# Spreading the small matmuls of a merged projection over more of its tiles

## The chip, the cores and the metric

The kernel runs on one core of a Trainium2 chip. Its engines are TensorE (PE), VectorE (DVE), ScalarE (ACT), GpSimd (POOL) and SyncE (SP, which issues the DMAs here). They run their own instruction streams and meet at semaphores. The metric is the time of one execution on the device in microseconds; before the change its median is 2121.88 us over 3 runs (2121.46 to 2122.12).

## The reference

Two transformer-like blocks follow each other on an input of 256 tokens by 1024 features. The second has two layers. Each starts with a layer norm and a mixer of three parts (SSD, RWKV-7 and gated linear attention), all fed by one projection `x @ w_in`; a mixture of experts follows. The part at stake is the projection with the RWKV mixer:

```python
def hybrid_mixer(x, w_in, ...):
    p = x @ w_in
    s_z, s_xbc, s_dt, rw, gq, gk, gv, gg, ga = _split(p, IN_SPLITS_2)
...
def rwkv7_mixer(p, mu, w0, w2, a0, a2, g2, k_k, k_a, r_k, ln_g, ln_b):
    prev = jnp.pad(p, ((0, 0), (1, 0), (0, 0)))[:, :seq]
    p = p + (prev - p) * mu
...
    def step(state, inp):
        r_t, w_t, k_t, v_t, kk_t, a_t = inp
        sa = jnp.einsum('bhvk,bhk->bhv', state, -kk_t)
        state = (state * w_t[:, :, None, :] + sa[..., None] * (kk_t * a_t)[:, :, None, :]
                 + v_t[..., None] * k_t[:, :, None, :])
        return state, jnp.einsum('bhvk,bhk->bhv', state, r_t)
```

## The kernel before, in words

The stage at stake is `stage_mix2` (L1254). It stands in a hardware loop over the two layers, so it runs twice; I call the runs the first and the second pass. The first starts near 646 us of the span, the second near 1380. Before and behind it all engines meet at a barrier.

**The projection.** The output features are cut into 24 tiles (units), in the order LOW, K0, K1, R0, R1, V0, V1, GA, GQ, GK, GG0, GG1, X0 to X0+5, TOKA, TOKB, Z0 to Z0+3. The first 12 are plain fp32: 8 matmuls of 128x128 by 128x256 (L1897). From X0 on, weights and input are split into a high and a low part, and a tile is 24 matmuls (L1900). Weights come through a ring of 4 buffers (`Units`): SP loads, ACT rounds to the high part (`round`, L1227), DVE subtracts for the low part (`rest`, L1233).

**The RWKV recurrence** is computed in chunks of 32 tokens by small matmuls. `products` (L1699) makes the masked products of the vectors of a chunk. `squares` (L1724, L1727) and `inverse` (L1738) build the inverse of a triangular 32x32 matrix per chunk and head by repeated squaring; DVE adds each update (L1405) and ACT copies each power. `transposes` (L1709) turns vectors to token order. `through` (L1746) applies the inverse. `states_and_ends` (L1765, L1768, L1771) and `read_out` (L1788, L1791, L1793) prepare the step from chunk to chunk, `state` (L1806, L1813) does the seven steps. `heads64` (L1687) sums over the 64 features of a head.

**The order** is written by hand. Each engine has a function `after(u)`: what it does behind tile u. PE runs tile u, then its `after(u)`, then tile u+1, and so on; the small matmuls of one `after` stand in one piece between two tiles. Only three updates of the state stand in the middle of a tile: `state(2)`, `state(4)`, `state(6)` in X0+3, X0+4, X0+5. ACT copies each tile out of PSUM (`copied`), and two banks take turns, so tile u waits for the copy of tile u-2.

**What depends on what.** `inverse(j)` needs power j+1 copied by ACT and update j-1 added by DVE. `through` into W1 and W2 needs update 3. The states need both copies of W (`w_copied`), one by ACT (L1637), one by DVE (L1486). The read-out needs Q and E, which DVE makes behind the states (L1494, L1497). State c needs DVE's state c-1 (L1412).

Of the kernel before, what the change touches and what calls it, by code (L numbers as in the profile page):

```python
# [22 lines left out]
ALU = mybir.AluOpType  # L23
# [6 lines left out]
DT = D // P  # L30
# [1223 lines left out]
def stage_mix2(nc, k, L, w_dram, v_dram, ln_dram, lr_dram, wa2_dram, vecs, b, y):  # L1254
# [6 lines left out]
    with Stage(nc, "mix2") as st:  # L1261
# [88 lines left out]
        with nc.Block() as block:  # L1350
# [16 lines left out]
            def _(dve):  # L1367
# [49 lines left out]
                def after(u):  # L1417
# [38 lines left out]
                    elif u == V1_:  # L1456
                        mask(2, mM[:, 0], "c_above")
# [4 lines left out]
                    elif u == GA:  # L1462
                        inverse(0)
# [3 lines left out]
                    elif u == GQ:  # L1467
                        inverse(1)
# [6 lines left out]
                    elif u == GK:  # L1475
                        inverse(2)
                        dve.wait_ge(masked_done, 5)
                        mask(3, mM[:, 1], "c_upto")
                        mask(4, mM[:, 2], "c_upto")
                    elif u == GG0:  # L1480
                        inverse(3)
                        dve.wait_ge(bonus_done, 1)
                        ch.link(dve.tensor_tensor(flat(v_), ps[:, 2], flat(v_), ALU.mult))
                    elif u == GG1:
                        dve.wait_ge(w_done, 1)
                        dve.tensor_copy(W12[:, 1].rearrange("p b h c -> p (b h c)"), ps[:, 5]).then_inc(w_copied, 1)  # L1486
# [3 lines left out]
                        ch.link(dve.tensor_scalar(x1[:], x1[:], 1.0 / 16, None, ALU.mult))  # L1490
                        dve.tensor_tensor_scan(gcum[:], k.c("keep")[:, 0:S], x1[:], 0.0, ALU.mult, ALU.add).then_inc(cums_ready, 1)
                    elif u == X0:
                        dve.wait_ge(qe_done, 1)
# [7 lines left out]
                    elif u == X0 + 1:  # L1501
# [4 lines left out]
                    elif u == X0 + 2:  # L1506
# [4 lines left out]
                    elif u == X0 + 3:  # L1511
                        state(2)
                        for t in range(2):
                            ins = dve.tensor_scalar(v_[:, t], v_[:, t], vec("ln_b", t), None, ALU.add)
                        ch.link(ins)
                        dve.wait_ge(gate_copied, 1)
                        dve.tensor_tensor(v_, v_, gg[:], ALU.mult).then_inc(vb_ready, 1)
                        state(3)
                    elif u == X0 + 4:
                        state(4)  # L1520
                        dve.wait_ge(vb_ready, 1)
                        for t in range(2):
                            dve.tensor_scalar(gg[:, t], gg[:, t], vec("ln_g", t), None, ALU.mult).then_inc(vb_ready, 1)
# [1352 lines left out]
```

## Time and profile before

| what | value |
|---|---|
| median of the runs | 2121.88 us |
| the profiled execution, its own time | 2135.11 us |
| its span, first to last instruction | 2133.8 us |
| PE busy | 1892.1 us, 89% |
| DVE busy | 830.4 us, 39% |
| ACT busy | 635.1 us, 30% |
| DMA, mean | 253 GB/s |
| stage of the change, first pass | about 646 to 791.5 us |
| stage of the change, second pass | about 1380 to 1532.5 us |

PE's busy time counts pipelined matmuls from start to modelled end, so a gap between two rows is real idle time while a busy row is not full speed. "issue" as a releaser means that the engine waited for nothing that the profile shows. PEclk is the clock that was granted to TensorE, 1.00 for 2.4 GHz, 0.50 for 1.2 GHz. The line numbers are those of the kernel before; in the kernel after, L1897 is L1898 and L1900 is L1901, and the lines of the helpers are 3 lower.

### The profile page before, as it was taken

The page shows a single profiled execution, that of the slowest core. Times are in us where ns is not written, and L with a number is a line of the kernel's source. Part 1 is how long each engine was busy: PE and PEld are TensorE (multiplying, and loading weights), DVE is VectorE, ACT ScalarE, POOL GpSimd, SP SyncE. Part 2 cuts the span into 40 slices and gives each one's busy share as a digit, 9 for nine tenths or more (in the row PEclk, how much of TensorE's full clock was granted, in tenths as well). Part 3 has the DMA queues.
Part 4 walks back from the last instruction along what each step waited for, and adds up shares of the span by engine and source line. Part 5 has one row for each costly group of instructions (what it writes and reads, how often), then busy time and mean ns, then how long its engine had stood idle before and what let it go on. Part 6 is the DMA issues. An engine that isn't in the chain of part 4 may idle for free. (4 is left out here: it accounts for less than half of the span.)

```text
span 2133.8 us, 41370 instructions
## 1 busy us (share of the span) xinstructions
PE 1892.1 (89%) x17744; PEld 1332.8 (62%) x17744; DVE 830.4 (39%) x1665; ACT 635.1 (30%) x1197; POOL 52.1 (2%) x58
## 2 busy tenths in 40 slices
PE   7999998999987886789999999588866999999995
PEld 6889998889986784644444444267855444444432
DVE  5766666666654375521111111233745111111112
ACT  4554445554433232311111111132423111111112
POOL 0400000400000000000000000000000000000000
PEclk9999999999998997799999999888977999999998
DMA  6235553345513312699999999422117999999992
GB/s 262 100 139 184 192 181 132 110 149 193 182 60 103 101 42 79 260 383 426 429 428 428 428 428 428 190 80 92 31 80 308 384 427 428 428 428 428 430 426 115
DMA packets 52332, 540.00 MB, mean 253 GB/s; under 512 B 6576, under 2 KB 7760, under 8 KB 14672
## 3 DMA queue, kind: packets, MB, share of 16 engines
q1 hardware_dynamic: 52176, 537.80, 63.0%
q8 instruction: 113, 1.85, 0.4%
q14 instruction: 43, 0.35, 0.1%
HBM read 536.73 MB, written 1.05 MB: 252 GB/s over the span
## 5 line engine op out<-in xcount | busy, mean ns | idle before, releaser
L2668 PE MATMUL experts_psG<-weights_gu,experts_xc 128*64 128x512 f32 x2048 | 454.5, 593 | 19.5 <-DMA weights_gu<-in_moe_up 19.5
L2668 PEld LDWEIGHTS experts_psG<-weights_gu,experts_xc 128*64 128x64 f32 x2048 | 146.9, 137 | 315.6 <-issue 277.2
L422 DVE TENSOR_TENSOR ring_low<-ring_raw,ring_high 128x1024 fp32r<-128x1024 f32 x180 | 224.3, 1248 | 158.3 <-ACT ring_high L416 158.2
L2693 PE MATMUL experts_psD<-weights_d,experts_hT 128*64 128x512 f32 x1024 | 233.9, 598 | 1.6 <-ACT experts_hT L2629 1.6
L416 ACT ACTIVATE ring_high<-ring_raw 128x1024 fp32r<-128x1024 f32 x180 | 189.1, 1054 | 155.0 <-PE ffn_ps L539 91.3
L537 PE MATMUL ffn_ps<-first_x_high,ring_high 128*128 128x256 f32 x704 | 199.0, 283 | 0.1
L2599 DVE SCALAR_TENSOR_TENSOR experts_yc_low<-experts_psD,experts_slot_gate,experts_yc_high 128x512 fp32r<-128x512 f32 x64 | 48.0, 751 | 387.7 <-ACT experts_yc_high L2632 387.7
L539 PE MATMUL ffn_ps<-first_x_high,ring_low 128*128 128x256 f32 x704 | 198.6, 282 | 0.0
L538 PE MATMUL ffn_ps<-first_x_low,ring_high 128*128 128x256 f32 x704 | 198.0, 281 | 0.0
L2589 DVE TENSOR_TENSOR experts_sig<-experts_sig,experts_psG 128x256 f32<-128x256 f32 x64 | 27.0, 421 | 370.0 <-ACT experts_sig L2620 370.0
L2620 ACT ACTIVATE experts_sig<-experts_psG 128x256 f32<-128x256 f32 x64 | 24.6, 384 | 420.1 <-PE experts_psG L2668 420.1
L2693 PEld LDWEIGHTS experts_psD<-weights_d,experts_hT 128*64 128x64 f32 x1024 | 68.4, 136 | 119.4 <-issue 111.2
L538 PEld LDWEIGHTS ffn_ps<-first_x_low,ring_high 128*128 128x128 f32 x704 | 134.2, 191 | 0.1
L537 PEld LDWEIGHTS ffn_ps<-first_x_high,ring_high 128*128 128x128 f32 x704 | 133.4, 189 | 0.9 <-issue 0.9
L539 PEld LDWEIGHTS ffn_ps<-first_x_high,ring_low 128*128 128x128 f32 x704 | 133.8, 190 | 0.0
L2632 ACT ACTIVATE experts_yc_high<-experts_psD,experts_slot_gate 128x512 fp32r<-128x512 f32 x64 | 44.0, 687 | 263.4 <-PE experts_psD L2693 263.4
L1897 PE MATMUL mix_ps<-x_resid,mix_w_raw 128*128 128x256 f32 x384 | 100.7, 424 | 14.4 <-issue 9.9
L2644 PE MATMUL experts_psX<-experts_selb,parts_x 128*128 128x64 bf16 x3072 | 102.2, 194 | 10.8 <-DVE experts_gate_e L2569 10.8
L2644 PEld LDWEIGHTS experts_psX<-experts_selb,parts_x 128*128 128x128 bf16 x3072 | 95.7, 99 | 11.0 <-DVE experts_gate_e L2569 11.0
L1897 PEld LDWEIGHTS mix_ps<-x_resid,mix_w_raw 128*128 128x128 f32 x384 | 81.8, 216 | 30.2 <-issue 17.0
L529 PE MATMUL ffn_ps<-ffn_act_high,ring_low 128*128 128x256 f32 x352 | 98.6, 280 | 0.0
L527 PE MATMUL ffn_ps<-ffn_act_high,ring_high 128*128 128x256 f32 x352 | 98.2, 279 | 0.0
(487 smaller groups left out, 3234.0 us busy)
## 6 DMA issues: line engine op xcount, KB each, us to landing
weights_gu<-in_moe_gate SPq DMA_DIRECT2D x64, 2048.0 KB, 25.1
weights_gu<-in_moe_up SPq DMA_DIRECT2D x64, 2048.0 KB, 29.5
weights_d<-in_moe_down SPq DMA_DIRECT2D x64, 2048.0 KB, 28.4
ring_raw<-in_w SPq DMA_DIRECT2D x90, 1024.0 KB, 4.9
mix_w_raw<-in_w_in SPq DMA_DIRECT2D x44, 512.0 KB, 3.7
output_w_raw<-in_w_out SPq DMA_DIRECT2D x8, 1024.0 KB, 8.1
mix_w_raw<-in_w_in SPq DMA_DIRECT2D x4, 528.0 KB, 5.4
const<-in_const SPq DMA_DIRECT2D x1, 1344.0 KB, 17.7
```

The costliest lines, as they stand in the source:

```text
L416: act.activation(self.high[:, n % AHEAD], self.raw_half(n), ACT.Copy).then_inc(self.rounded, 1)
L422: dve.tensor_tensor(self.low[:, n % AHEAD], self.raw_half(n), self.high[:, n % AHEAD], ALU.subtract)\
L527: pe.matmul(out, w[0][:, kk], high, start=False, stop=False)
L529: return pe.matmul(out, w[1][:, kk], high, start=False, stop=stop)
L537: pe.matmul(out, w[0][:, kk], f.high[:, kk], start=kk == 0, stop=False)
L538: pe.matmul(out, w[0][:, kk], f.low[:, kk], start=False, stop=False)
L539: ins = pe.matmul(out, w[1][:, kk], f.high[:, kk], start=False, stop=kk == DT - 1)
L1897: return pe.matmul(out, a, c, start=kc == 0, stop=kc == DT - 1)
L2599: dve.scalar_tensor_tensor(yc_low[:], psD[:], slot_gate[:, par:par + 1], yc_high[:], ALU.mult, ALU.subtract)\
L2644: ins = pe.matmul(psX[:, t * SLOTS:(t + 1) * SLOTS], m.parts[:, i, blk, t * P:(t + 1) * P], selb[:, par, blk, 0:SLOTS], start=i == 0 and b ...
L2668: ins = pe.matmul(out, xc[:, kk], wgu[:, place, kk, :, j * S:(j + 1) * S], start=kk == 0, stop=kk == DT - 1)
L2693: ins = pe.matmul(psD[rows, :], hT[:, c, j * SLOTS:(j + 1) * SLOTS], wd[:, place, 2 * j + c, i * 512:(i + 1) * 512], start=j == 0 and c == ...
```

## The change

Two things move. The pieces of the recurrence are handed out to the tiles anew, most of them one tile later: `products(2)` and `mask(2)`, the four updates of the inverse, `products(4)`, the last two transposes, `through`, the states, the read-out, all state steps and the normalization behind them. And a function `within(u)` is new: what PE does in the middle of tile u. It takes `products(2)` (GA), `inverse(0)` to `inverse(3)` (GQ, GK, GG0, GG1), the first half of `states_and_ends` (X0+1) and the three even state steps. DVE and ACT follow in their `after` functions. No operation is added or dropped. PE's part of the diff:

```diff
@@ tensor
-                def states_and_ends():
+                def states_and_ends(ns):
                     pe.wait_ge(w_copied, 2)
-                    for n in range(NP):
+                    for n in ns:
...
                     elif u == V1_:
                         pe.wait_ge(masked, 2)
                         squares(0)
-                        pe.wait_ge(gate_copied, 1)
-                        pe.wait_ge(F_ready, 3)
-                        products(2, K_, A_)
                     elif u == GA:
                         squares(1)
-                        inverse(0)
                         transposes(0, F[:, A_])
                         transposes(1, F[:, B_])
                     elif u == GQ:
                         squares(2)
-                        inverse(1)
...
                     elif u == GK:
                         squares(3)
-                        inverse(2)
                         pe.wait_ge(abs_ready, 1)
                         pe.wait_ge(F_ready, 4)
                         products(3, B_, R_)
+                    elif u == GG0:
+                        pe.wait_ge(masked, 4)
                         products(4, K_, R_)
                         transposes(2, F[:, K_])
                         transposes(3, v_)
-                    elif u == GG0:
-                        inverse(3)
+                    elif u == GG1:
...
-                    elif u == X0:
-                        states_and_ends()
                     elif u == X0 + 1:
+                        states_and_ends(range(NP // 2, NP)).then_inc(qe_done, 1)
+                    elif u == X0 + 2:
                         read_out()
-                    elif u == X0 + 2:
-                        state(1)
...
+                def within(u):
+
+                    if u == GA:
+                        pe.wait_ge(gate_copied, 1)
+                        pe.wait_ge(F_ready, 3)
+                        products(2, K_, A_)
+                    elif u in (GQ, GK, GG0, GG1):
+                        inverse(u - GQ)
+                    elif u == X0 + 1:
+                        states_and_ends(range(0, NP // 2))
+                    elif u in (X0 + 4, X0 + 5, TOKA):
+                        state(2 * (u - X0 - 3))
...
-                            if kc == DT // 2 and X0 + 2 < u < TOKA:
-                                state(2 * (u - X0 - 2))
+                            if kc == DT // 2:
+                                within(u)
```

DVE and ACT, the pieces that the prediction speaks of:

```diff
@@ vector
                     elif u == GA:
-                        inverse(0)
+                        mask(2, mM[:, 0], "c_above")
...
                     elif u == GQ:
-                        inverse(1)
+                        inverse(0)
...
                     elif u == X0:
+                        dve.wait_ge(w_done, 1)
+                        dve.tensor_copy(W12[:, 1].rearrange("p b h c -> p (b h c)"), ps[:, 5]).then_inc(w_copied, 1)
...
@@ scalar
-                    elif u == GG1:
+                    elif u == X0:
                         act.wait_ge(w_done, 1)
                         act.activation(W12[:, 0].rearrange("p b h c -> p (b h c)"), ps[:, 4], ACT.Copy).then_inc(w_copied, 1)
...
-                    elif u == TOKB:
+                    elif u == Z0:
                         act.wait_ge(var_done, 1)
                         ch.link(act.activation(flat(lnv[:]), ps[:, 3], ACT.Ln, bias=k.eps[64e-5], scale=1.0 / 64))
                         act.activation(rstd[:], lnv[:], ACT.Exp, scale=-0.5).then_inc(rstd_ready, 1)
```

PE from the squares behind tile V1 to the piece behind tile GQ. `mix_w_raw` rows are the tiles, `mix_mN` squares, `mix_mX` the inverse, `mix_rw_F 32x32` products, `const,mix_rw_F` transposes. Before:

```order
L1724 MATMUL mix_ps<-mix_mN 32x32 x32
L1727 MATMUL mix_ps<-mix_mN 32x32 x32
L1699 MATMUL mix_ps<-mix_rw_F 32x32 x32
L1897 MATMUL mix_ps<-x_resid,mix_w_raw 128x256 x8
L1724 MATMUL mix_ps<-mix_mN 32x32 x32
L1727 MATMUL mix_ps<-mix_mN 32x32 x32
L1738 MATMUL mix_ps<-mix_mX,mix_mN 32x32 x32
L1709 MATMUL mix_ps<-const,mix_rw_F 128x128 x8
L1897 MATMUL mix_ps<-x_resid,mix_w_raw 128x256 x8
L1724 MATMUL mix_ps<-mix_mN 32x32 x32
L1727 MATMUL mix_ps<-mix_mN 32x32 x32
L1738 MATMUL mix_ps<-mix_mX,mix_mN 32x32 x32
```

And now:

```order
L1721 MATMUL mix_ps<-mix_mN 32x32 x32
L1724 MATMUL mix_ps<-mix_mN 32x32 x32
L1898 MATMUL mix_ps<-x_resid,mix_w_raw 128x256 x4
L1696 MATMUL mix_ps<-mix_rw_F 32x32 x32
L1898 MATMUL mix_ps<-x_resid,mix_w_raw 128x256 x4
L1721 MATMUL mix_ps<-mix_mN 32x32 x32
L1724 MATMUL mix_ps<-mix_mN 32x32 x32
L1706 MATMUL mix_ps<-const,mix_rw_F 128x128 x8
L1898 MATMUL mix_ps<-x_resid,mix_w_raw 128x256 x4
L1735 MATMUL mix_ps<-mix_mX,mix_mN 32x32 x32
L1898 MATMUL mix_ps<-x_resid,mix_w_raw 128x256 x4
L1721 MATMUL mix_ps<-mix_mN 32x32 x32
```

Products 2 moved from behind V1 into the middle of GA, the inverse from behind its squares into the middle of the next tile.

DVE around tiles GG1, X0 and X0+1. The `mix_w_low` rows are the splits of the weights; before, these are units 14, 15 and 16:

```order
L1233 TENSOR_TENSOR mix_w_low<-mix_w_raw,mix_w_high 128x1024
L1486 COPY mix_W<-mix_ps 128x512
L1487 TENSOR_SCALAR mix_x<-mix_x 128x256
L1489 TENSOR_TENSOR mix_x<-mix_x 128x256
L1490 TENSOR_SCALAR mix_x<-mix_x 128x256
L1491 SCALAR_TENSOR_TENSOR mix_gcum<-const,mix_x 128x256
L1233 TENSOR_TENSOR mix_w_low<-mix_w_raw,mix_w_high 128x1024
L1494 TENSOR_TENSOR mix_wa<-mix_ps,const 128x1024
```

And now, from the last update of the inverse:

```order
L1405 TENSOR_TENSOR mix_mX<-mix_mX,mix_ps 128x256
L1486 SCALAR_TENSOR_TENSOR mix_gcum<-const,mix_x 128x256
L1488 TENSOR_TENSOR shifted<-mix_ps,shifted 128x512
L1233 TENSOR_TENSOR mix_w_low<-mix_w_raw,mix_w_high 128x1024
L1491 COPY mix_W<-mix_ps 128x512
L1493 TENSOR_SCALAR shifted<-shifted,vecs 128x256 x2
L1496 TENSOR_TENSOR shifted<-shifted,mix_gg 128x512
L1233 TENSOR_TENSOR mix_w_low<-mix_w_raw,mix_w_high 128x1024
L1500 TENSOR_SCALAR mix_gg<-mix_gg,vecs 128x256 x2
L1502 TENSOR_TENSOR mix_wa<-mix_ps,const 128x1024
```

The copy of W stood ahead of the split of unit 15 and now stands behind it.

## Rows read from the trace of the kernel before

**Rows 1.** Waits of PE, 655 to 792 us: us in total, times, longest

```profile
PE mix_ps L1897 <- issue: 4.5, 2, 2.6
PE mix_ps L1699 <- issue: 3.0, 1, 3.0
PE mix_ps L1738 <- issue: 2.3, 1, 2.3
...
PE mix_ps L1768 <- issue: 2.1, 1, 2.1
PE mix_ps L1806 <- DVE mix_ex L1412: 1.1, 1, 1.1
PE mix_ps L1900 <- ACT z L1678: 0.7, 1, 0.7
```

**Rows 2.** Waits of PE, 1392 to 1532 us

```profile
PE mix_ps L1897 <- issue: 5.4, 2, 2.8
PE mix_ps L1738 <- issue: 4.2, 1, 4.2
...
PE mix_ps L1768 <- issue: 1.9, 1, 1.9
```

**Rows 3.** A stretch between gaps: length, busy us and count of each engine, clock, DMA

```profile
688.95:701.50 12.55, 12.37 (x383) 10.28 (x382) 2.17 (x5) 1.78 (x4) 0.00 (x0) 0.86 0.21 51
```

**Rows 4.** DMA queues, 685.5 to 747 us: packets, MB, share

```profile
q8 instruction: 12, 0.20, 1.2%
```

**Rows 5.** PE in order of time, first pass: start, us, operation, count [idle before]

```profile
685.03 1.30 PE L1699 MATMUL mix_ps<-mix_rw_F 64*32 64x32 f32 x128
688.98 5.30 PE L1897 MATMUL mix_ps<-x_resid,mix_w_raw 128*128 128x256 f32 x16 [2.64 <-issue]
...
705.99 4.18 PE L1897 MATMUL mix_ps<-x_resid,mix_w_raw 128*128 128x256 f32 x16
...
715.34 3.07 PE L1897 MATMUL mix_ps<-x_resid,mix_w_raw 128*128 128x256 f32 x13 [1.89 <-issue]
...
736.35 1.10 PE L1746 MATMUL mix_ps<-mix_cum,mix_mX 32*32 32x64 f32 x64
...
746.65 0.39 PE L1900 MATMUL mix_ps<-mix_xs_high,mix_w_high 128*128 128x256 f32 x1
746.88 0.28 PE L1900 MATMUL mix_ps<-mix_xs_low,mix_w_high 128*128 128x256 f32 x1
...
749.70 0.80 PE L1788 MATMUL mix_ps<-mix_mM,mix_W 32*64 32x32 f32 x60
```

**Rows 6.** PE in order of time, second pass

```profile
1439.47 0.68 PE L1738 MATMUL mix_ps<-mix_mX,mix_mN 32*32 32x32 f32 x33 [4.18 <-issue]
...
1441.85 4.89 PE L1897 MATMUL mix_ps<-x_resid,mix_w_raw 128*128 128x256 f32 x16
1446.66 0.72 PE L1724 MATMUL mix_ps<-mix_mN 32*32 32x32 f32 x62
...
1447.80 0.74 PE L1738 MATMUL mix_ps<-mix_mX,mix_mN 32*32 32x32 f32 x64
...
1452.81 5.65 PE L1897 MATMUL mix_ps<-x_resid,mix_w_raw 128*128 128x256 f32 x13 [2.80 <-issue]
...
1463.91 0.29 PE L1699 MATMUL mix_ps<-mix_rw_F 64*32 64x32 f32 x14 [2.99 <-issue]
1464.13 0.66 PE L1709 MATMUL mix_ps<-const,mix_rw_F 128*128 128x128 f32 x4
...
1465.23 5.14 PE L1897 MATMUL mix_ps<-x_resid,mix_w_raw 128*128 128x256 f32 x16
```

**Rows 7.** A stretch of the second pass, columns as in rows 3

```profile
1437.58:1444.40 6.82, 4.93 (x47) 4.34 (x48) 1.30 (x3) 1.20 (x2) 0.00 (x0) 0.50 0.01 2
```

**Rows 8.** DVE in order of time, first pass

```profile
738.41 0.69 DVE L1486 COPY mix_W<-mix_ps 128x512 f32<-128x512 f32 x1 [1.66 <-PE mix_ps L1746]
...
742.55 1.23 DVE L1233 TENSOR_TENSOR mix_w_low<-mix_w_raw,mix_w_high 128x1024 fp32r<-128x1024 f32 x1 [1.74 <-ACT mix_w_high L1227]
```

More of the change, by code:

```diff
@@ L1510, in after @@
                         state(1)
[L1511 to L1523, printed above, removed]
-                        state(5)
-                    elif u == X0 + 5:
+                    elif u in (X0 + 4, X0 + 5):
+                        state(2 * (u - X0 - 3))
+                        state(2 * (u - X0 - 3) + 1)
+                    elif u == TOKA:
                         state(6)
@@ L1539, in after @@
                     elif u == Z0:
+                        convolve((4, 5))
+                    elif u == Z0 + 1:
                         dve.wait_ge(vb_ready, 3)
@@ L1629, in after @@
                         act.activation(x2[:], x2[:], ACT.Ln, bias=k.eps[1.0]).then_inc(ln_ready, 1)
+                    elif u == GG0:
                         to_tokens(2)
                         to_tokens(3)
-                    elif u == GG0:
+                    elif u == GG1:
                         act.wait_ge(mv_done, 1)
                         act.activation(W0.rearrange("p b h c -> p (b h c)"), ps[:, 3], ACT.Copy).then_inc(mv_copied, 1)
-                    elif u == GG1:
-                        act.wait_ge(w_done, 1)
-                        act.activation(W12[:, 0].rearrange("p b h c -> p (b h c)"), ps[:, 4], ACT.Copy).then_inc(w_copied, 1)
                         act.wait_ge(cums_ready, 1)
@@ L1640, in after @@
                         act.activation(en[:], gcum[:], ACT.Exp, scale=-1.0).then_inc(g_exps_ready, 1)
-                    elif u == X0 + 1:
+                    elif u == X0:
+                        act.wait_ge(w_done, 1)
+                        act.activation(W12[:, 0].rearrange("p b h c -> p (b h c)"), ps[:, 4], ACT.Copy).then_inc(w_copied, 1)
+                    elif u == X0 + 2:
                         act.wait_ge(rp_ready, 1)
@@ L1861, in after @@
                         transposes(3, v_)
-                    elif u == GG0:
-                        inverse(3)
+                    elif u == GG1:
                         pe.wait_ge(tok_copied, 4)
@@ L1868, in after @@
                         heads64(2, t1, ones64).then_inc(bonus_done, 1)
-                    elif u == GG1:
+                    elif u == X0:
                         pe.wait_ge(inv_updated, 4)
```

56 lines of the change are left out of this document (31 added, 25 removed).

## The prediction, made before the kernel was run

> **What bounds the kernel now.** I read the waits of PE first. PE is busy 89% of the span (the table of the profile), and both passes of the merged projection lie between barriers of all engines, so a microsecond of PE saved there is saved in the whole. In the first pass PE's idle time there has almost no releaser: 4.5 us ahead of L1897, 3.0 ahead of L1699, 2.3 at L1738, 2.1 at L1768, all "issue"; DVE and ACT hold PE for 1.1 and 0.7 us only [rows 1]. The second pass: 5.4, 4.2 and 1.9, and 3.0 at L1699 [rows 2, 6]. That is 11.9 and 14.5 us, 13.2 a pass, in gaps that no semaphore explains. So the change cannot gain by covering latencies of DVE or ACT: those are covered already.
>
> What are the gaps? Count instructions between them. From the end of one gap to the start of the next stand 383 matmuls and 382 weight loads, 765 together [rows 3]: 3 times 256, less a few semaphore instructions. And the instruction queue q8 moved 12 packets, 0.20 MB, in the stretch from 685.5 to 747 us, in which PE went through 12 times 256 instructions [rows 4]: about 65 bytes each. So code comes in blocks of 256 instructions, and PE stops where one is not there. A gap follows a block that ran fast: the 256 instructions of products 0 and 1 start at 685.03 and the next block at 688.98, 3.95 us later, of which 2.64 are idle [rows 5].
>
> The Trainium skill ("Runtime: NRT & Kernel Launch", Instruction fetch mechanics) also says that code is refilled in blocks of 256 instructions, the next while the current one runs, but that crossing a boundary is "mostly hidden". By that the gaps would have another cause and the change would move none of them; the multiple of 256 and the gaps of 2 to 4 us speak against it.
>
> The second loss is the clock. After such gaps PE runs at half speed: between 1437.58 and 1444.40 the granted clock is 0.50, that is 1.2 instead of 2.4 GHz [rows 7]. At full speed 13 matmuls of a tile (L1897) take 3.07 us, so its 16 take 3.65 without the last one's tail; they took 5.30 and 4.18 after gaps of the first pass [rows 5]; in the second 4.89, 5.65 for only 13, and 5.14 [rows 6].
>
> **The change, part by part.** It adds and removes no matmul; PE issues 4536 instructions in this stage before and after, so all later code keeps its place in its blocks. It moves work between blocks. One fp32 matmul of the program is two loads and two matmuls on PE, so an fp32 tile is 32 instructions, a piece of 32 small products 128. Prices at full clock: tile 3.65 us; 256 of squares 1.14 (1446.66 to 1447.80; I price the inverse alike); products 0.65 per 128, half of 1.30; `through` about 0.95 per 128, from 1.10 with its tail; 8 transposes, 16 instructions, 1.1 (1464.13 to 1465.23) [rows 5, 6]. States and read-out I take at 0.007 and 0.006 us an instruction, near `through`; an f32r tile at 3.0 (746.65 to 749.70), its half at 1.5.
>
> Cut into blocks of 256 from the one that ends in the gap at 686.4, the work in us is, before: 1.5, 4.5, 4.75, 1.15, 5.7, 1.8, 4.0, 1.4, 5.9, 6.1, 4.4, 1.8, 4.2, 3.5. Block 4, for instance, is 193 instructions of squares and 62 of the inverse: nothing else. After: 1.5, 4.5, 4.75, 3.9, 2.9, 2.9, 3.0, 4.8, 5.8, 5.3, 3.1, 3.1, 4.3, 1.5. Block 5 is now 99 of the inverse (0.5), half a tile (1.8) and 141 of squares (0.6). The last one is new on the wrong side: 256 instructions that are all read-out.
>
> A block cannot pass faster than the next one arrives. That time is 3.95 us in the case above, and longer elsewhere: the gap at 1439.47 alone is 4.18 [rows 6], with the squares and the inverse of its block before it some 5.5. At 4.1 us the blocks of before fall short by 2.6+2.95+2.3+0.1+2.7+2.3+0.6 = 13.6 us, close to the 13.2 read, so I take 4.1. Those of after fall short by 2.6+0.2+1.2+1.2+1.1+1.0+1.0+2.6 = 10.8. Gain: 2.8 a pass, **5.6 us**. At 3.5 us it would be 3.5 a pass, at 5.5 it would be 1.6, so this term is between 3 and 7.
>
> Clock: the gap behind products 0 and 1 stays where it is, with its slow tile (1.6 us). The other slow tiles cost 0.5 and some 1.6 (transposes, later tile) in the first pass, and 1.2, 2.6, 1.5 and some 1.7 (transposes, states) in the second, 9 in all [rows 5, 6]. The new gaps are 1.0 to 1.2 instead of 2 to 4 us and lie between half tiles. The clock held through a gap of 1.89 us in the first pass (13 matmuls in 3.07 us behind it) [rows 5] and fell at longer ones, so I take half back, **4.5 us**; ends 0 and 9. In blocks that wait for code anyway a low clock costs only what exceeds 4.1 us.
>
> Switches: six pieces now stand inside a tile. The first f32r matmul behind states takes 0.39 instead of 0.28 and its next starts 0.23 behind it [rows 5], so a switch in and out is about 0.2, 1.2 a pass; four of the six lie in blocks with slack. Cost **0.8 us**, at most 2.4. The Trainium skill ("TensorE: Matmul & The Clock Gate", Part 3, what overlaps and what doesn't) says that a weight load passes running matmuls only where their row groups differ, so each change between full tiles and small ones exposes a load. By that the cost exists in all six; the row gives its size.
>
> The end: PE waits 0.7 us for ACT's copy of z [rows 1], since ACT loads a table and finishes the normalization ahead of that copy. These steps now come a tile later, ahead of the copy of Z0+1, which only Z0+3 needs. Gain 0.7 a pass, **1.4 us**. The 1.1 us wait for DVE L1412 stays: convolve, qt, kt and the first state move by one tile together with what PE does.
>
> New waits: inverse(j) in the middle of a tile asks for the sum j-1 that DVE does right behind the previous tile, with squares and half a tile between, over 2 us for one 0.4 us operation. Behind the wait on PE stand half a tile and all that follows, so a late sum would show at once. The thin place is X0+1: the first half of the states wants W12, half an f32r tile (1.5) after `through` instead of a whole one. DVE must first split unit 15, which now stands ahead of the copy; in the trace it ends at 742.55 + 1.23 = 743.8, 7.4 us behind the end of tile GG1 (736.35); then the 0.69 us copy [rows 5, 8], 8.1. PE comes there 0.95 (`through`) + 1.0 (sum of the bonus) + 3.0 (X0) + 1.9 (`through` twice) + 1.5 = 8.35 behind it. It fits by 0.2; I take 0, and up to 2 a pass if the weights land late.
>
> SP's queue of weight loads is released by the same tiles in the same order; its 0.5 MB loads keep their distance.
>
> Sum: -5.6 - 4.5 + 0.8 - 1.4 = -10.7, rounded to **-10 us**. The profiled execution took 2135.11 us with a span of 2133.8, so it would become 2125. The runs without a profile have a median 13.2 us lower, 2121.88; the same difference gives **2112 us**, if the gaps are as large without a profile.
>
> **The rivals.**
> A. The clock stays low through the dense middle (blocks 4 to 8). Every half tile there costs 1.8 more and the transposes 1.1: blocks of 6.8, 4.7, 4.7, 4.8 and 8.4 us, 29.4 against the 21.2 that they take at full clock and arrival every 4.1. A pass loses 8.2 and gains 2.8 of gaps and the 4.5 that the clock costs today; with switches and the end about +1 in all, 2123. For it: the clock was low for 6.8 us on end in the second pass [rows 7]. Against: in the first pass it was back at once.
> B. The gaps do not depend on what a block holds, as the page says, or the saved gap time comes back in other blocks: 0, 2122. Against: all long gaps follow a block of small products.
> C. Slower. Arrival is later in the new pattern. A block entered without a gap before it has waited longer for its successor (5.5 us) than one entered out of a gap (3.95). After the change fewer blocks are entered fresh. If arrival takes 5.0 us throughout, the blocks of after lack 19.7 us against the 13.2 read, +13 in both passes, less the 4.5 of the clock and 0.6 of the rest: +8, 2130. It loses from about 4.7 us on. The new read-out block alone then costs 3.5 a pass. For it: the second pass. Against: in the first, such blocks took 3.6 to 4.6.
>
> **How the numbers follow.** About 0.2% is what a measurement of this kernel tells from no change, 4.2 us. Forecast 0.66, A 0.14, B 0.09, C 0.11. The forecast's own range is 2103 to 2119; a little of it is within 0.2%. A is split over the three; C is mostly slower. Faster 0.72, same 0.19, slower 0.09. The range 2102 to 2123 leaves out C and the far end of the clock term.
>
> **What would show it.** Right: the gaps at L1738 and L1699 gone or under 1.5 us, gaps of about 1 to 1.5 us inside squares, inverse and products 3; the gap after products 0 and 1 unchanged; a new gap of 2 to 3 us at or behind the read-out; 10 to 11 us of "issue" a pass; tiles GQ to GG1 at 1.8 us a half; no wait of PE on ACT's z. Wrong: PE waiting for DVE L1405 or L1491, a granted clock of 0.5 from GQ to GG1, or "issue" at 13 us a pass as now.

## The result, and the profile after

The kernel after takes 2101.56 us (median of 4 runs, 2093.48 to 2102.97) against 2121.67 (4 runs, 2118.86 to 2122.12) before: ratio 0.990, interval 0.9874 to 0.9927. The forecast was 2112, its range ended at 2102; the direction is right, the size is not: 20 us instead of 10. In a later set of runs the same kernel gave 0.9935 (0.9917 to 0.9952), 2099.88 against 2115.00. So the change is worth 14 to 20 us. The profiled execution took 2100.94 us, span 2099.6.

Two passes of the kernel after, one stretch each; the columns are those of [rows 3], the seventh group is the granted clock:

```profile
652.70:776.60 123.90, 116.93 (x2230) 101.90 (x2230) 66.78 (x132) 47.85 (x83) 0.00 (x0) 0.96 0.29 87
1376.30:1499.60 123.30, 117.17 (x2230) 102.11 (x2230) 66.79 (x132) 48.01 (x83) 0.00 (x0) 0.96 0.29 88
```

The same stretches of the kernel before, from its first tile to its last:

```profile
658.80:790.10 131.30, 117.01 (x2230) 103.11 (x2230) 66.41 (x132) 47.99 (x83) 0.00 (x0) 0.95 0.27 82
1392.70:1530.80 138.10, 121.97 (x2230) 106.66 (x2230) 66.40 (x132) 47.98 (x83) 0.00 (x0) 0.90 0.26 78
```

Length less PE busy is idle time: 14.3 and 16.1 us before, 7.0 and 6.1 after. PE busy fell by 4.9 in all, nearly all of it in the second pass, whose clock was 0.90. What is left of PE's waits, first pass (us in total, times, longest; "issue" where the profile shows nothing that PE waited for):

```profile
PE mix_ps L1898 <- issue: 2.5, 1, 2.5
PE mix_ps L1898 <- ACT x_resid L220: 2.2, 1, 2.2
PE mix_ps L1788 <- issue: 2.0, 1, 2.0
PE mix_ps L1765 <- issue: 0.9, 1, 0.9
PE mix_ps L1735 <- issue: 0.8, 1, 0.8
PE mix_ps L1762 <- issue: 0.5, 1, 0.5
PE mix_ps L1696 <- issue: 0.4, 1, 0.4
```

Against [rows 1] the 3.0 us at the products (L1699, now L1696) are 0.4, the 2.3 at the inverse (L1738, now L1735) are 0.8, the 2.1 in the states (L1768, now L1765) are 0.9; the waits for DVE L1412 and for ACT's z are gone. (The 2.2 us for L220 is the start of the pass.) New is the wait at L1788, the read-out. PE in order of time, columns as in [rows 5]:

```profile
678.89 1.30 PE L1696 MATMUL mix_ps<-mix_rw_F 64*32 64x32 f32 x128
682.66 5.30 PE L1898 MATMUL mix_ps<-x_resid,mix_w_raw 128*128 128x256 f32 x16 [2.46 <-issue]
...
697.60 0.75 PE L1735 MATMUL mix_ps<-mix_mX,mix_mN 32*32 32x32 f32 x64
698.29 1.99 PE L1898 MATMUL mix_ps<-x_resid,mix_w_raw 128*128 128x256 f32 x8
...
705.44 0.25 PE L1735 MATMUL mix_ps<-mix_mX,mix_mN 32*32 32x32 f32 x5 [0.77 <-issue]
705.63 1.99 PE L1898 MATMUL mix_ps<-x_resid,mix_w_raw 128*128 128x256 f32 x8
...
709.28 0.29 PE L1696 MATMUL mix_ps<-mix_rw_F 64*32 64x32 f32 x14 [0.41 <-issue]
```

The first gap, behind products 0 and 1, and the slow tile behind it are nearly what they were [rows 5]: 3.77 us from the start of the products to the next block, 5.30 for the tile. All half tiles from GQ to GG1 stand at full clock (1.99 us with the tail of the last matmul). The gaps between them are 0.4 and 0.8 us (in the second pass one of 1.3), where the forecast had five of 1.0 to 1.2 in the whole pass.

All kernels that ran, with the passes of their profiled executions (first / second). Length runs from the start of the first tile to the end of the last. Gaps are PE's idle times over 0.3 us between the two, waits for other engines included, good to some 0.2 us a pass; slow is the time at 1.2 GHz, in the clock rows of the trace. These three columns are of one execution each:

| kernel | median, ratio to before (interval) | length | gaps | slow |
|---|---|---|---|---|
| before | 2121.67 | 131.3 / 138.1 | 14.1 / 15.6 | 14 / 27 |
| before again | 2118.58, one run | 129.7 / 133.0 | 13.2 / 14.6 | 14 / 17 |
| after | 2101.56, 0.990 (0.9874-0.9927) | 123.9 / 123.3 | 6.8 / 5.9 | 10 / 10 |
| after again | 2099.88, 0.9935 (0.9917-0.9952) | 122.8 / 122.5 | 4.9 / 5.8 | 10 / 10 |
| inverse moved alone | 2099.88, 0.9943 (0.9922-0.9965) | 123.8 / 121.0 | 7.2 / 7.1 | 10 / 3 |
| spread, nothing mid-tile | 2106.50, 0.9962 (0.9944-0.998) | 128.2 / 124.8 | 10.6 / 9.7 | 17 / 10 |
| before + fill | 2118.53, 1.0029 (1.001-1.0047) | 129.4 / 130.2 | 7.4 / 7.4 | 7 / 7 |
| before, small loads | 2104.44, 0.9951 (0.9932-0.997) | 126.5 / 123.5 | 10.9 / 9.9 | 10 / 7 |
| after, shifted | 2102.04, 0.9937 (0.9918-0.9957) | 122.8 / 122.3 | 3.8 / 6.1 | 10 / 3 |
| after, two blocks thinned | 2098.82, 0.9923 (0.9899-0.9947) | 121.9 / 122.0 | 5.1 / 5.5 | 7 / 7 |
| the same, DVE reordered | 2094.38, 0.9915 (0.9892-0.9937) | 117.7 / 118.0 | 2.0 / 2.8 | 3 / 3 |
| after, double loads | 2114.16, 1.0004 (0.9983-1.0025) | 123.9 / 126.0 | 7.4 / 9.5 | 10 / 10 |
| after, small loads | 2097.45, 0.9934 (0.9909-0.9958) | 123.1 / 119.9 | 6.0 / 4.5 | 10 / 7 |

The runs of before beside them had medians of 2115.00 (rows 4 to 7 of the table), 2116.82 (before again, both 8th to 10th) and 2113.27 (the last three), each over 17 to 25 runs. As before itself moved by that much between sets of runs, rows are compared by their ratios and not by their medians.

### The profile page after: what moved, and what is told of

Same layout as the page of the kernel before. It is cut to its first block and busy times, and to the rows that moved or that the text cites. A ratio compares the mean times of both kernels' runs of the same rounds, so it can differ in the third digit from the quotient of the medians.

```text
span 2099.6 us, 41370 instructions
## 1 busy us (share of the span) xinstructions
PE 1877.0 (89%) x17744; PEld 1319.1 (63%) x17744; DVE 830.2 (40%) x1665; ACT 635.1 (30%) x1197; POOL 53.2 (3%) x58
## 5 line engine op out<-in xcount | busy, mean ns | idle before, releaser
L2647 PE MATMUL experts_psX<-experts_selb,parts_x 128*128 128x64 bf16 x3072 | 102.2, 194 | 10.8 <-DVE experts_gate_e L2572 10.8
L1898 PE MATMUL mix_ps<-x_resid,mix_w_raw 128*128 128x256 f32 x384 | 96.2, 406 | 9.3 <-issue 4.8
L528 PE MATMUL ffn_ps<-ffn_act_low,ring_high 128*128 128x256 f32 x352 | 98.2, 279 | 0.0
```

The source lines that it names most:

```text
L528: pe.matmul(out, w[0][:, kk], low, start=False, stop=False)
L1898: return pe.matmul(out, a, c, start=kc == 0, stop=kc == DT - 1)
L2647: ins = pe.matmul(psX[:, t * SLOTS:(t + 1) * SLOTS], m.parts[:, i, blk, t * P:(t + 1) * P], selb[:, par, blk, 0:SLOTS], start=i == 0 and b ...
```

## The experiments

Theory T throughout: PE waits for its next block of 256 instructions. Its refinement T2, formed on the traces of the first four: the request for that block waits behind a weight load issued ahead of it. The crossing is the moment at which the first instruction of a block runs; the request is the start of the next 16 KB packet on q8, the queue that carries the code.

**1. The kernel after, once more.**

> The changed kernel once more, timed beside the others and with a second trace. Both theories: about 20 us below the kernel before (0.990). Theory T (PE waits for blocks of 256 instructions, and the clock falls behind gaps of 2 us and more): gaps at the same instructions as in the first trace of this kernel, 6 to 7 us a pass. Rival W (the gaps come from waits between engines that the trace doesn't show): gaps at other places, or of other size by more than 2 us a pass.

Ratio 0.9935, gaps 4.9 and 5.8 us a pass. The gain repeats, at its lower end: 14 us where 20 were expected, and both passes have less than the expected 6 to 7 us of gaps. All the gaps stand at instructions that have one in the first trace. Between two executions of one kernel the gaps of a pass can thus differ by 1.9 us, nearly what rival W had asked for; it is experiment 7 that speaks against W.

**2. Only the inverse moved.** The kernel before; PE's four updates go to the middle of GQ, GK, GG0 and GG1, DVE's sums one tile later:

```diff
                     elif u == GA:
                         squares(1)
-                        inverse(0)
...
+                            if kc == DT // 2 and u in (GQ, GK, GG0, GG1):
+                                inverse(u - GQ)
                             if kc == DT // 2 and X0 + 2 < u < TOKA:
```

> The kernel before, with one thing changed: the four updates of the inverse stand in the middle of the next tile, on PE, and behind it on DVE. Products, states, read-out and all else stay with their tiles. Theory T: blocks of 256 in the middle then hold half a tile each; work of them at least 2.9 us instead of 1.2 and 1.3; gaps of 5 to 7 us a pass instead of 13, clock up in the middle. So nearly the whole gain: 14 to 20 us below before. Rival S (what counts is that the pieces are spread over more tiles): under 8 us of gain.

0.9943, or 12 us, a little less than the expected 14 to 20 and not to be told from the whole change. The gaps at the inverse and at the products fell to 0.7 and 0.4, those that this edit doesn't touch stayed: 2.1 in the states, 1.0 for DVE L1412, 0.7 for ACT's z.

```profile
PE mix_ps L1768 <- issue: 2.1, 1, 2.1
PE mix_ps L1806 <- DVE mix_ex L1412: 1.0, 1, 1.0
PE mix_ps L1738 <- issue: 0.7, 1, 0.7
PE mix_ps L1896 <- ACT z L1678: 0.7, 1, 0.7
PE mix_ps L1699 <- issue: 0.4, 1, 0.4
```

**3. Spread, but nothing in the middle of a tile.** The kernel after with `within(u)` called behind the tile, ahead of `after(u)`:

```diff
-                            if kc == DT // 2:
-                                within(u)
...
+                    within(u)
                     after(u)
```

> The changed kernel with nothing in the middle of a tile: what it did there is done behind that tile, ahead of the rest (the three even state steps too, which also the kernel before had in the middle). Theory T: the pieces are as dense as before, gaps of 10 to 13 us a pass, two of them over 2 us in the middle with a slow clock behind; 0 to 8 us below before. Rival S: 14 to 20 us below before, like the changed kernel.

0.9962. Gaps of 1.6 in the squares and 3.4 in the products in the first pass: two pieces in a row again make a block of small matmuls alone. The later tiles by themselves bring about half (8 us; the intervals of the two ratios overlap).

**4. Work that nobody reads, as filler.** The kernel before, with four fp32 matmuls of 128x256 in each of four dense places a pass (64 PE instructions, 7.4 us of PE's work a pass, output overwritten):

```diff
+                def fill(u):
+                    pe.wait_ge(copied, in_turn(u + 1) - 1)
+                    for _ in range(4):
+                        pe.matmul(ps[:, bank(u + 1), 0:S], ones64, k.x[:, 0], start=True, stop=True)
```

> The kernel before with work added: four times a pass, 4 matmuls of 128x128 by 128x256 whose result nobody reads, inside the dense pieces (between squares and inverse behind GA and GQ, between products 3 and 4, in the middle of the states). That is 64 more instructions and 7.4 us more of PE work a pass, 14.8 in all. Theory T: the added work stands where PE waited for code, gaps fall from 13 to 6 or 7 us a pass, and the clock stays up there: -4 to +6 us against before. Rival W, or any theory in which the gaps don't depend on what a block holds: +12 to +17 us.

1.0029, about 6 us for 14.8 us of added work. Gaps fell to 7.4 a pass, the slow time from 41 (or 31) to 14. So more than half of the work went into time in which PE stood still or slow. That rules out gaps of a fixed length. It doesn't rule out unseen waits for other engines, which work put ahead of them would have shortened in the same way; experiment 7 does that.

**5. The kernel before, once more.**

> The kernel before, once more under the profiler, to see which of its gaps repeat. Theory T (PE waits for its next block of 256 instructions, and the block's request waits for a weight load that was issued just ahead of it): the same five or six places of the instruction stream have the gaps, behind products 0/1, in the inverse, behind the third update, in products 3 and in the states; gaps of PE over 0.3 us sum to 13 to 16 us a pass; where a weight load lies between the crossing into a block and the request for the next, the gap is 2 us longer than where none does, in either pass. The low clock adds up to 14 to 28 us a pass. Rival (the 14.1 and 15.6 us of the first profile are a disturbed execution, as that one took 13 us more than its median): gaps sum to 9 to 11 us a pass here, near the 10.6 that the move of the inverse alone would then have to win from.

Same places, 13.2 and 14.6 us. The gap in the inverse is 2.2 and 3.1, against 2.3 and 4.2. The time at 1.2 GHz is 31 us in place of 41. The execution that the prediction was built on took 13 us more than the median, and those 10 us at the lower clock were part of that. That a load ahead makes the gap in the inverse 2 us longer was not seen here: in the second pass only 19 of its packets stood ahead of the request, which came 1.40 us behind the crossing against 0.83 in the first, and 0.3 us of the 0.8 that the gap was longer lie behind the request.

**6. Small loads.** In the kernel before, units 8 to 17 fetch 32 columns of a weight tile instead of all; PE, ACT and DVE work on what the buffers hold, so these tiles' values are left out:

```diff
-                    w.load(sp, i, w_dram[bass.ds(L, 1), :, off:off + UNIT_SIZES[i]]...)
+                    if not 8 <= i < 18:
+                        w.load(sp, i, w_dram[bass.ds(L, 1), :, off:off + UNIT_SIZES[i]]...)
+                    else:
+                        w.load(sp, i, w_dram[bass.ds(L, 1), :, off:off + 32]..., 32)
```

> The kernel before, but the weight loads of tiles GQ to X0+5 (units 8 to 17) fetch 16 KB instead of 0.5 MB; PE, ACT and DVE do exactly what they did, on what the buffers held, so these tiles' values are left out. T2 (the request for a block waits behind a weight load; 3.4 to 3.8 us from crossing to arrival without one, 4.5 to 5.6 with one): in blocks where 121 to 144 load packets started between the crossing and the request, the delay to the request falls from 2.2 to 3.3 us to 0.8 to 1.5; the gap in the inverse of 4.2 us in the second pass becomes 1.7 to 2.5, that behind the third update 1.3 to 1.9; gaps sum to 9 to 11.5 us a pass in both passes instead of 14.1 and 15.6; with the clock that comes back the time falls by 5 to 12 us, ratio 0.994 to 0.998. Rival (the request is late for a reason of PE's own, since it also has values of 2.5 and 2.9 us with no load packets in between): delays and gaps stay within 0.5 us, time within 0.1% of before. Second rival (T1 of the prediction, arrival at a constant 4.1 us): the same as no change.

This is the run that settles that a load ahead delays the request. Take the block whose first instruction runs at 1447.26 in the second pass of before. First what the DMA queues did from there to 1450.5, then from 1450.5 to 1451.6 (packets, MB, share of the 16 engines):

```profile
q1 hardware_dynamic: 143, 0.52, 56.6%
```

```profile
q8 instruction: 1, 0.02, 5.4%
q1 hardware_dynamic: 1, 0.00, 0.1%
```

The request for the next block (q8, 16 KB) starts at 1450.55, when the load of 0.5 MB is through. PE gets on at 1452.81, 5.5 us after it entered the block, with the 2.80 us gap of [rows 6]. The same block with small loads is entered at 1427.13. The queues from 1427.13 to 1428.30, and from there to 1429.40:

```profile
q1 hardware_dynamic: 142, 0.02, 9.2%
```

```profile
q8 instruction: 1, 0.02, 5.4%
q1 hardware_dynamic: 2, 0.00, 0.1%
```

```profile
1430.74 3.07 PE L1900 MATMUL mix_ps<-x_resid,mix_w_raw 128*128 128x256 f32 x13 [0.79 <-issue]
```

As many packets stand ahead, but short ones: the request starts 1.18 us behind the crossing instead of 3.29, PE gets on after 3.6 us, the gap is 0.79 instead of 2.80. From request to the next instruction it is 2.3 us in one and 2.4 in the other.

The Trainium skill ("DMA: Bandwidth & Descriptors", Queues, rings and completion order) says that a DMA engine goes round its queue rows and drains a whole packet of some 9 to 17 descriptors before it switches. The load's 144 pieces over 16 engines are 9 each, and here the code request did wait for all of them, which agrees. In experiment 10 one waited for some 360, 23 for each engine, more than a packet of that usual size.

The gap in the inverse of the second pass: 1.7 instead of 4.2 and 3.1; behind the third update 0.7 and 0.8 instead of 1.9 and 2.8. All in the expected range or below it. The median is 12 us lower, 10 by the ratio.

The number of load packets ahead does not give the delay by itself. In before the block entered at 1482.16 has 136 of them started between crossing and request, and the request comes after an ordinary 1.23 us; the one entered at 723.83 has none, and its request comes after 2.49 us. Such late requests without a load held up no block here (that block has 7.3 us of work); why they are late is not shown.

**7. Everything shifted by half a block.** The kernel after, with 32 products of one chunk repeated ahead of products 0:

```diff
+                        for n in range(32):
+                            pe.matmul(ps[0:C, 0, 0:C], F[0:64, A_, 0, 0:C], F[0:64, B_, 0, 0:C], start=True, stop=True, tile_position=(0, 0))
                         products(0, A_, B_)
```

> The kernel after, with 32 products of a chunk repeated ahead of products 0 (128 more instructions on PE, results overwritten, some 0.65 us of work a pass), so that every later instruction stands half a block further back. T: no gap of over 0.7 us stands behind products 0/1 any more, since the 256 instructions of the products no longer fill one block; gaps stand instead in the piece of products 2 and squares (0.5 to 1.2 us each), at the tile behind squares 3 (1.2 to 1.8) and in the read-out piece (1.2 to 1.8), all at positions that are 17 over a multiple of 256 of this stage's stream; sum 4.5 to 8 us a pass; the clock falls less often behind products 0/1. Time 2096 to 2104, within 0.3% of the kernel after. Rival (a gap belongs to its piece, by a semaphore, a switch of tile shapes or PE's own queue): the 2.3 us gap stays between products 1 and the tile behind it, and the read-out's at its last instruction.

PE in the first pass, from the repeated products (L1832) on:

```profile
680.81 1.30 PE L1832 MATMUL mix_ps<-mix_rw_F 64*32 64x32 f32 x36
...
681.96 0.77 PE L1696 MATMUL mix_ps<-mix_rw_F 64*32 64x32 f32 x61
683.26 0.74 PE L1696 MATMUL mix_ps<-mix_rw_F 64*32 64x32 f32 x63 [0.54 <-issue]
683.93 3.72 PE L1900 MATMUL mix_ps<-x_resid,mix_w_raw 128*128 128x256 f32 x16
...
690.72 0.54 PE L1696 MATMUL mix_ps<-mix_rw_F 64*32 64x32 f32 x39
692.66 0.33 PE L1696 MATMUL mix_ps<-mix_rw_F 64*32 64x32 f32 x25 [1.40 <-issue]
```

The gap between products 1 and the tile (2.5 and 2.3 us in after) is gone, and with it the slow tile (3.72 instead of 5.30). Gaps now stand inside pieces: 63 matmuls ahead of the end of products 1, and 39 matmuls into products 2, in the middle of runs of matmuls without a wait. All "issue" gaps over 0.3 us, of both passes, are at places 17 over a multiple of 256 of the stage's PE stream. Time 0.9937, like after. The sizes were met in part: the gap in products 2 is 1.4 and 1.7 where 0.5 to 1.2 were expected, and the first pass sums to 3.8, below the range. A gap belongs to a block, not to a piece.

**8. The two densest blocks thinned.** The kernel after, products 1 in the middle of V1 and the second half of the read-out in the middle of X0+3 (DVE does its shift of V0 ahead of the masks, which now come later, and PE's first squares wait for the sum behind the masks):

```diff
                         products(0, A_, B_)
-                        products(1, B_, A_)
...
+                    if u == V1_:
+                        products(1, B_, A_)
...
+                    elif u == X0 + 3:
+                        read_out((1,))
```

> The kernel after with its two densest blocks thinned: products 1 goes to the middle of tile V1 (DVE masks both products a tile later), and the second half of the read-out to the middle of X0+3. T: the gap behind products 0/1 (2.3 us) becomes two of 0.4 to 1.0, the one behind the read-out (1.5 to 2.0) becomes 0.5 to 1.0; gaps sum to 3.5 to 5 us a pass instead of 5.9 to 6.8; the low clock behind products 0/1 goes or is halved (1.6 us a tile). Time 3 to 8 us under the kernel after, 2092 to 2098 if that is 2100 here, ratio to before 0.988 to 0.992. Rival A (the masks come too late at their new place): PE waits for DVE ahead of squares 0, 0.5 to 2 us a pass, and the time is like after, 2100. Rival B (a gap costs nothing but is bookkeeping of the trace): 2100.

0.9923 and 2098.82 us, just outside the expected 0.988 to 0.992 and 2092 to 2098. The gaps behind products 0/1 (2.3 to 2.5) and the read-out (1.5 to 2.0) are 0.7 us or less, as expected; but a wait for DVE's state stands in their place, which none of the rivals named at this place:

```profile
PE mix_ps L1803 <- DVE mix_ex L1412: 2.6, 1, 2.6
PE mix_ps L1901 <- ACT x_resid L220: 2.2, 1, 2.2
PE mix_ps L1696 <- issue: 1.1, 2, 0.7
```

DVE shows why. It waits for the later read-out, and only then has 0.7 us of the sum, 3.4 of a convolution that needs nothing of it, and the rest:

```profile
739.55 0.69 DVE L1511 TENSOR_TENSOR mix_rk<-mix_rw_F,mix_ps 128x512 f32<-128x512 f32 x1 [4.10 <-PE mix_ps L1790]
740.15 0.73 DVE L1383 TENSOR_SCALAR cx<-xbc,vecs 128x256 f32<-128x256 f32 x2
740.92 2.71 DVE L1388 SCALAR_TENSOR_TENSOR cx<-xbc,vecs,cx 128x256 f32<-128x256 f32 x6
```

**9. The same, with DVE reordered.**

```diff
                     elif u == X0 + 2:
+                        convolve((0, 1))
                         dve.wait_ge(rp_done, 2)
                         dve.tensor_tensor(by_chunk(Rp[:]), ...).then_inc(rp_ready, 1)
-                        convolve((0, 1))
```

> The version before this one (products 1 in the middle of V1, half of the read-out in the middle of X0+3), with one thing more: DVE does convolve(0, 1), 3.4 us that need nothing of the read-out, ahead of its sum of Rp and not behind it. In the run before, DVE waited 4.1 us for the read-out, then did the sum (0.7), convolve (3.4), a split (1.25), qt and kt (0.75) and the state, and PE waited 2.6 us for that state. T: that wait goes (DVE has its 3.4 us while it waits), gaps sum to 2.5 to 3.5 us a pass, and the slow tile behind it goes with it; time 4 to 9 us under the run before, 2090 to 2095 at before's 2117, ratio 0.988 to 0.9905. Rival: the wait of 2.6 us is on the read-out's second half itself; it stays, time as before this edit, 2099.

```profile
736.42 2.71 DVE L1388 SCALAR_TENSOR_TENSOR cx<-xbc,vecs,cx 128x256 f32<-128x256 f32 x6
739.59 0.69 DVE L1512 TENSOR_TENSOR mix_rk<-mix_rw_F,mix_ps 128x512 f32<-128x512 f32 x1 [0.45 <-PE mix_ps L1790]
```

```profile
654.40:772.10 117.70, 114.87 (x2230) 99.46 (x2230) 66.96 (x132) 47.81 (x83) 0.00 (x0) 0.99 0.29 92
1374.60:1492.60 118.00, 114.67 (x2230) 99.38 (x2230) 66.92 (x132) 47.76 (x83) 0.00 (x0) 0.99 0.29 92
```

The wait fell from 2.6 to 1.0 us and did not go. Both passes are near 118 us, 4.5 to 6.3 shorter than in either execution of after, with gaps of 2.0 and 2.8 us; inside the passes the clock is low only in the 3.4 us at the start. 2094.38 us, 0.9915: the best of all. It misses the expected 0.988 to 0.9905, and its interval overlaps that of after again. The traces show the two passes 10 to 12 us shorter than in after, but the whole span only 5 (2095.0 against 2099.6 and 2100.0): outside the passes this execution took 5 to 7 us more. So the passes are faster than those of after; that the whole kernel is faster is likely but not shown.

**10. Double loads.** The kernel after, each load of units 8 to 17 followed by a second of the same 0.5 MB into a spare buffer:

```diff
+                    if 8 <= i < 18:
+                        if i > 8:
+                            sp.wait_ge(spare_loaded, 16 * (i - 8))
+                        sp.dma_start(spare[:], w_dram[...]).then_inc(spare_loaded, 16)
```

> The kernel after, with each weight load of tiles GQ to X0+5 (units 8 to 17) followed at once by a second one of the same 0.5 MB into a spare buffer that nothing reads. PE, ACT and DVE do the same. T2 (a block's request goes out behind the load packets ahead of it): 288 packets instead of 108 to 144 stand ahead of the requests of 785, 1553, 2065 and 2577, their delay grows from 1.8 to 2.9 us to 4 to 6, the gap behind block 1553 (0.76 and 1.28 us) becomes 3 to 4, new ones of 1 to 2.5 us appear at 1041, 2321 or 2833, gaps sum to 10 to 15 us a pass, and the time rises by 8 to 18 us to 2108 to 2118, to about the kernel before. Rival (load packets do not delay a request; what shortened the gaps in the run with small loads was free memory bandwidth, DMA busy share 0.2): delays within 0.5 us of after, time within 3 us of 2100.

1.0004: the whole gain is gone, although order and compute are those of after. In the profiled execution the block entered at 1455.05, which had 17 load packets ahead of its request in after, has these up to 1459.35, and then this gap:

```profile
q1 hardware_dynamic: 359, 1.36, 93.6%
```

```profile
1461.68 0.25 PE L1791 MATMUL mix_ps<-mix_mM,mix_W 32*64 32x32 f32 x4 [2.10 <-issue]
```

The delay of that request is 4.4 us (4.6 in the first pass), in a block for which nothing was expected. At the four blocks named ahead it is 2.4 to 3.3 us where 4 to 6 were expected, the gap behind block 1553 (the one in the inverse) is 0.9 and 1.8 instead of 3 to 4, and gaps sum to 7.4 and 9.5, less than the expected 10 to 15. That execution was the fastest of its 12 (2101.59), 12.6 us under their median. Its two passes are 2.6 to 4.6 us longer than those of the two executions of after, so the trace shows the mechanism and a third or less of the price. Where the rest of the 14 us arises was not seen; the second loads also hold up the weight loads behind them.

**11. Small loads in the kernel after.** The edit of experiment 6 on the kernel after.

> The kernel after, with the weight loads of units 8 to 17 cut to 16 KB as in the run with the kernel before; those tiles' values are left out. T2: in the kernel after only the gap behind block 1553 stands behind a load (delays 2.4 and 2.9 us), so little is left to win: gaps fall from 6.8 and 5.9 to 4 to 5.5 us a pass, the gaps behind products 0/1 (2.3) and behind the read-out (1.5 to 2.0) stay, since no load is ahead of them; time 1 to 5 us under after, 2095 to 2099. With the 12 us that the same cut gave the kernel before, this would say that half of what the change won was to get requests out of the loads' way. Rival (what the loads cost has nothing to do with the order of the pieces): the same 10 to 14 us less as in the kernel before, 2088.

0.9934, the ratio of after itself (0.9935). The gap behind block 1553 (blocks go by the place of their first instruction in the stage's PE stream; this is the 0.8 and 1.3 us gap in the inverse) is gone, those behind products 0/1 (2.5, 1.9) and the read-out (1.7, 1.4) stay, as expected. The time in us is in the expected range only because before was faster beside it, too; by the ratios nothing was won, with an uncertainty of 0.3%. The same cut gave before 0.9951.

## Why the prediction was half right

**The failed step** is the size of the gap term, 5.6 us forecast and 11.7 or more measured. It is in the part that priced the gaps: "A block cannot pass faster than the next one arrives. ... At 4.1 us the blocks of before fall short by ... 13.6 us, close to the 13.2 read, so I take 4.1." One constant was fitted to a sum. But the arrival depends on whether a load stands ahead of the request:

| block entered | load packets ahead of the request | crossing to request | crossing to next block's first instruction, where PE waited |
|---|---|---|---|
| before 700.01, first pass | 0 | 0.92 us | 3.6 |
| before 1433.97, second pass, same block | 144 | 3.29 | 5.5 |
| before 1447.26 | 144 | 3.29 | 5.5 |
| small loads 1427.13, same block | 144, short | 1.18 | 3.6 |
| after 1417.37 | 7 | 1.03 | block was long enough |

(The first two rows are the 2.3 us of [rows 1] and the 4.18 of [rows 6]: the same block, with other gaps because of where the load fell.) The table has the shortest and the longest. Over both traces of before, where PE stood still: 3.4 to 3.9 us with at most 14 load packets ahead of the request, 4.4 with 19, and 4.4 to 5.6 with 118 to 144 (the gaps in the inverse, behind the third update and in products 3). The block ahead of the gap in the states does not fit: 3.5 to 4.0 with 95 to 136. With 3.5 my own formula gives 3.5 us a pass for the move (redone, 3.4: the shortfalls of after at 4.1 us add up to 10.9 and not 10.8). Experiments 6 and 11 measure that part: with the loads out of the way, code gaps sum to 9.3 and 8.1 us in before and to 6.0 and 4.5 in after, 3.4 a pass (7.1 us for both by the lengths of the passes; by the ratios, 0.9951 and 0.9934, 4 us with an uncertainty of 7). The rest comes from a sentence that was priced at nothing: "SP's queue of weight loads is released by the same tiles in the same order; its 0.5 MB loads keep their distance." They keep it to the tiles, not to the crossings of blocks. Before, loads cost 3.5 us of gaps a pass (12.2 in experiment 5 against 8.7 in 6), after 1.1 (6.4 against 5.3), or 0.1 with the second trace of after (5.4). So 2.4 to 3.8 us more a pass (the larger against the first trace; 1 us more each with the second trace of after) were won by getting requests out of the loads' way. Experiment 10 takes the whole gain away again, though its trace shows only a part of how. Rival C had the right variable, an arrival that varies from case to case, and the wrong sign.

**The gap term**, 5.6 us forecast, is 11.7 us against experiment 5 and 14.6 against the first trace, both passes, and 2 us more each with the second trace of after. That is the miss.

**Clock and switches**, forecast -4.5 and +0.8. Together they are the change of PE's busy time: 239.0 to 234.1, -4.9, against the first trace; 234.4 to 234.1, -0.3, against the second. The sum of -3.7 lies between. "Half back" was wrong in kind: in the middle, GQ to GG1, all of it came back in all four passes of the two executions of after, and what is left stands behind products 0/1, behind the read-out and at the start of each pass. Rival A (slow through the dense middle) was not seen in any of them. The 0.8 of switches was not measured by itself.

**The end**, 1.4 us: ACT's z no longer holds PE, in both passes. Right.

**"The 1.1 us wait for DVE L1412 stays":** wrong. It is in none of the four passes of after, and it was worth 1.4 to 2.1 us. Where the gap at the read-out is thinned away it comes back, 2.6 us (experiment 8) and 1.0 (9), so in after that gap seems to hide it by giving DVE the time; no run tests this alone, and in experiment 7 the wait is there in the second pass (1.2 us) beside a gap of 1.4.

**New waits**: none for L1405 or L1491, as forecast; the copy of W that fitted by 0.2 us fitted. The new gap at the read-out is 2.0 and 1.5, forecast 2.6, and that behind products 0/1 stayed, as forecast.

**Rival B**, by which the gaps would not move, is out: they went with the blocks in experiments 2, 3, 7 and 8, and shrank with added work in 4. So is, for this stream, the page of the Trainium skill ("Runtime: NRT & Kernel Launch", Instruction fetch mechanics) that holds a crossing to be mostly hidden: 12 to 15 us a pass of before were not hidden.

**The sum.** The two passes went from 269.4 us in the first trace, or 262.7 in the second, to 247.2: 22 or 15.5 us less. The runs say 20 and 14. The prediction was built on one execution only, and an unusually long one. Outside the two passes, where the kernels do not differ, its span has 1864.5 us against 1854.6 in the second trace of before, 1852.4 and 1854.8 in after and 1850.5 to 1859.4 in the others. So totals of single executions differ by up to 10 us for reasons that have nothing to do with the change, and a change of this size is read from the passes and from medians of many runs.

## What to carry to other kernels

On PE, small matmuls cost no less than their block of 256 instructions: a block of before that holds nothing else takes 1.2 to 1.5 us of work and at least some 3.5 of arrival. Cut the stream into blocks, put large matmuls into every block, and look at where big loads are issued relative to the crossings, since a request for code can wait for them. Don't fit one constant to a sum of gaps; look at the shortest and the longest and ask what was different there. And when a gap is closed, look at what it was covering on other engines.

## What the runs showed of the hardware that was not expected

- A code request can wait behind bulk loads: in the blocks of before behind which PE stood still, 0.8 to 1.6 us from crossing to request with few packets ahead, 1.9 to 3.3 with the whole load of 0.5 MB or nearly so, and 0.8 to 1.5 for the same blocks with the load cut to 144 short packets; up to 4.6 with more than one load (experiment 10). Exceptions both ways stand at experiment 6. From the start of the request to the next instruction it is 2.2 to 3.0 us with or without a load ahead, those of 2.6 and more where the packet of the request itself took 1.1 to 1.6 us instead of 0.9.
- The gap's length alone does not tell whether the clock falls: behind the start of the pass it held through 2.1, 2.2 and 1.9 us in the first pass of experiment 5 (it fell first behind the one of 2.99), while in the first pass of experiment 6 it fell behind gaps of 2.36 and 2.05 us and then held through one of 2.44.
- 14.8 us of added PE work cost 6 us (experiment 4), where it stood in front of such gaps.
